# Products of 256 columns paired into products of 512 in the FFNs and the MLP of a two-block transformer on one core

## The chip, the cores and the metric

The kernel runs on one core of a Trainium2 chip. The metric is the device time of one execution in microseconds, the median of several runs. Everything is computed in one launch; all inputs and the output are float32 in HBM.

## The reference

The input is one sequence of 256 tokens of width 1024. Two blocks follow each other. The first has sliding-window, top-k and memory attention, gates, and an MLP. The second has four SwiGLU FFNs, a gated chunk mixer and a sparse attention. The change touches only the MLP and the FFNs:

```python
h = rmsnorm(x, g_mlp[l])
hid = jnp.square(jax.nn.relu(jnp.einsum("bsd,df->bsf", h, w_mlp_in[l])))      # 1024 -> 4096
x = x + jnp.einsum("bsf,fd->bsd", hid, w_mlp_out[l])                          # 4096 -> 1024

def swiglu(x, w1, w3, w2):                                                    # 1024 -> 2816 -> 1024, four times
    return (jax.nn.silu(x @ w1) * (x @ w3)) @ w2
```

## The kernel before, in words

**Two parts for each number.** Every large product runs on TensorE in fp32r, and each operand is held as a high part (the rounded value) and a low part (what the rounding lost). A product is the sum of three: high weight by high activation, high weight by low, low weight by high (`passes`). The activations of a stage lie transposed in SBUF in `hT_hi` and `hT_lo` (128 features x 8 slices x 256 tokens each); the hidden values in `hid_hi` and `hid_lo`.

**Units.** Weights come as units of 1 MB (128 x 2048 floats), in one fixed order (`plan_units`). SyncE loads a unit into one of 3 ring slots; ScalarE rounds it into the high part of one of 3 split slots (`round_unit`, L1622); VectorE subtracts to get the low part (`low_unit`, L2113), which frees the ring slot; TensorE uses it and then frees the split slot for the unit three later. The last unit of a stage goes into a place of its own, `two`.

**Chunks.** The MLP has 16 chunks of 256 hidden features, each FFN 11. Per chunk an FFN takes the units w1, w3 and w2, the MLP the units mu and md. TensorE runs one chunk ahead: w1(c+1), w3(c+1), then the down product w2(c), which accumulates into banks 4 to 7 over all chunks. The middle chunks run in hardware loops of 2 (FFN) or 3 (MLP) chunks. Chunk 0 of three FFNs (`TOK`) and chunks 0 and 1 of the MLP are computed tokens first and are turned on TensorE; that is not changed, nor is chunk 0 of FFN 2.

**An up product** (`up_T_split`) computes 128 hidden features for 256 tokens: for each of 8 slices of the contraction three matmuls of 256 columns with 128 x 128 weights, all into the same 256 columns of a PSUM bank. `two_streams` interleaves the first and the second 128 tokens. So an FFN chunk has 96 up matmuls of 256 columns and 24 down matmuls of 512, an MLP chunk 48 and 24. In an FFN the bank holds the w1 sums in its left half and the w3 sums in its right, and there are two such tiles per chunk, over banks 0 to 3; in the MLP both halves of one bank hold the two feature tiles of a chunk, over banks 0 to 2. Banks are handed out by `plan_tiles`; TensorE waits on `tile_read` of a bank before it opens it.

**The hidden values.** ScalarE applies Silu (or Relu) from the bank into `act_out` (`activate`, L1797). VectorE multiplies that with the bank (L2560 in the FFNs, L2476 in the MLP), casts to the high part (L2457) and subtracts for the low part (L2459), and then makes the low parts of the next units. TensorE waits on `hid_ready` before the down product.

**The end of a stage** (`down_last`): after the last up product TensorE does 12 matmuls of the chunk before and then needs the last hidden chunk. In VectorE's program the low part of the unit for the next stage (`following`) stands ahead of the last hidden chunk. In FFN 0, eight transposes (`turn_ws`) stand between the last up product and the 12 matmuls.

Of the kernel before, what the change touches and what calls it, by code (L numbers as in the profile page):

```python
# [130 lines left out]
def plan_tiles():  # L131
# [10 lines left out]
    def ffn(f):  # L142
        out = [("f", f, c, t) for c in range(FFN_CHUNKS) for t in range(2)]
        return out[0:2] + [("ht", f)] + out[2:] if f in TOK else out
# [18 lines left out]
    names += [("m", 0), ("hm", 0), ("m", 1), ("hm", 1), ("rel",)] + [("m", c) for c in range(2, MLP_CHUNKS)]  # L163
# [9 lines left out]
    names += [("cr", 1)] + [("ch", 1, m) for m in range(2)] + third[2:]  # L173
# [153 lines left out]
def two_blocks(nc, t, out):  # L327
    ctx = ExitStack()
    with ctx:
# [22 lines left out]
        hT_hi = sb("hT_hi", [P, KT, S], F32R)  # L352
        hT_lo = sb("hT_lo", [P, KT, S], F32R)
# [163 lines left out]
        act_ready, hid_rounded, hid_ready = sem("act_ready"), sem("hid_rounded"), sem("hid_ready")  # L517
        ws_ready, sgu_var, sgu_sd, v_ready = sem("ws_ready"), sem("sgu_var"), sem("sgu_sd"), sem("v_ready")
# [285 lines left out]
        def _(pe):  # L804
# [341 lines left out]
            def mlp(n):  # L1146
# [31 lines left out]
                def chunk(c):  # L1178
                    have(("mu", c + 1))
                    o = open_tile(("m", c + 1))  # L1180
                    for f in range(2):
                        ins = up_T_split(o[:, f * S:(f + 1) * S], parts(("mu", c + 1), KT), f * P, P)
                    owed[0] += 1
                    ins.then_inc(tile_done, 1)
                    return down(c)

                def chunk_in_turn(k, i):

                    b, held, _ = TILES[("m", MLP_BODY + k + 1)]
                    pe.wait_ge(tile_read[b], i + (held - 1))  # L1190
                    unit = split_in_turn(("mu", 1), 2 * k, i, KT)
                    for f in range(2):
                        ins = up_T_split(banks[b][:, f * S:(f + 1) * S], unit, f * P, P)
                    owed[0] += 1
                    ins.then_inc(tile_done, 1)
# [29 lines left out]
            def ffn(f, between=None):  # L1225

                def up_w1(tiles, w1):
                    for ft in range(2):
                        up_T_split(tiles[ft][:, 0:S], w1, ft * P, P)
                    owed[0] += 1  # L1230

                def up_w3(tiles, w3):
                    for ft in range(2):
                        up_T_split(tiles[ft][:, S:2 * S], w3, ft * P, P).then_inc(tile_done, 1)
                    owed[0] += 1

                def first_by_features():
# [8 lines left out]
                    up_w3(tiles, parts(("w3", f, 0), KT))  # L1246
# [30 lines left out]
                def chunk(c):  # L1277

                    have(("w1", f, c + 1))
                    tiles = [open_tile(("f", f, c + 1, ft)) for ft in range(2)]  # L1280
                    up_w1(tiles, parts(("w1", f, c + 1), KT))
# [5 lines left out]
                    up_w3(tiles, parts(("w3", f, c + 1), KT))  # L1287
# [7 lines left out]
                def chunk_in_turn(k, i):  # L1295

                    tiles = []
                    w1 = split_in_turn(("w1", f, 1), 3 * k, i, KT)
                    for ft in range(2):
                        b, held, _ = TILES[("f", f, FFN_BODY + k + 1, ft)]  # L1300
                        pe.wait_ge(tile_read[b], i + (held - 1))
                        tiles.append(banks[b])
                    up_w1(tiles, w1)
                    up_w3(tiles, split_in_turn(("w1", f, 1), 3 * k + 1, i, KT))
# [292 lines left out]
        def _(act):  # L1597
# [201 lines left out]
            def mlp():  # L1799
                first = ("mu", 1)  # L1800
                seq = TILES[("m", 2)][2] + 1 - 2
# [17 lines left out]
                relu(2)  # L1819
                round_next(first, 5)  # L1820
                round_next(first, 6)
                with act.Fori(1, turns - 1) as i:
                    for k in range(MLP_BODY):
                        activate(TILES[("m", k)][0], i * MLP_BODY + (seq + k), ACT.Relu, 2 * S)
                        round_unit(first, i, 2 * k + 1)
                        round_unit(first, i, 2 * k + 2)
                for c in range(MLP_CHUNKS - 1 - MLP_BODY, MLP_CHUNKS - 1):
                    relu(c)
# [3 lines left out]
                relu(MLP_CHUNKS - 1)  # L1832
# [1119 lines left out]
```

## Time and profile before

| what | value |
|---|---|
| median of 3 runs | 1398.87 us (1398.53 to 1399.31) |
| the profiled execution | 1398.66 us |
| its span | 1396.9 us |
| granted TensorE clock | 0.995 of full speed |
| TensorE matmul, weight load | 98 %, 91 % of the span |
| VectorE, ScalarE | 67 %, 47 % of the span |
| DMA | 268.41 MB, mean 192 GB/s |

The span is what the profile covers from the first to the last instruction; 1.8 us lie around it. An engine's share is the time in which it had an instruction running. A matmul's duration overlaps that of the next, so the rate of TensorE is read from the distance between starts, not from durations.

### The profile page before, as it was taken

The numbers are of one execution on the slowest core, as the hardware profiler recorded it, in microseconds if no ns is written. First come the engines' busy times: TensorE is split into PE (matmuls) and PEld (weight loads), VectorE is DVE, ScalarE is ACT, GpSimd is POOL, SyncE is SP. The second block draws the span as 40 slices with busy tenths as digits, with TensorE's granted clock in tenths as the row PEclk, the third lists the DMA queues.
The fourth block names the chain that finished last, engine by engine and source line by source line (L and its number), as shares of the span: only waits on it lengthen the run. The fifth ranks groups of instructions, "written<-read, shape, count | busy, mean of one in ns | idle before, by whom it ended". The sixth has DMA issues, their size and how long they took to land.

```text
span 1396.9 us, 25172 instructions
## 1 busy us (share of the span) xinstructions
PE 1364.2 (98%) x10394; PEld 1274.9 (91%) x10394; DVE 938.3 (67%) x1372; ACT 657.8 (47%) x833; POOL 76.5 (5%) x73
## 2 busy tenths in 40 slices
PE   8999989999999999999999999999999999999997
PEld 7989978999999999999889999999999887899996
DVE  6778687656675555768885556666565667765566
ACT  5666544443443444454443434444433568543432
POOL 0000150000100000000030000100000200100000
PEclk8999999999999999999999999999999999999999
DMA  8434564776658767555466656766656530566551
GB/s 284 152 122 152 196 206 154 236 237 208 214 188 249 268 206 231 181 187 176 159 217 202 203 190 217 259 216 212 210 184 207 159 135 17 182 216 205 197 195 60
DMA packets 191526, 268.41 MB, mean 192 GB/s; under 512 B 5741, under 2 KB 164753, under 8 KB 191183
## 3 DMA queue, kind: packets, MB, share of 16 engines
q1 hardware_dynamic: 186336, 250.05, 54.6%
q0 software_dynamic: 4224, 15.91, 3.3%
q10 hardware_dynamic: 878, 1.21, 0.4%
q8 instruction: 64, 1.05, 0.3%
q14 instruction: 24, 0.19, 0.0%
HBM read 261.92 MB, written 4.19 MB: 190 GB/s over the span
## 4 chain that ended last, share of the span: by engine, by line
PE 80%; DVE 12%; ACT 4%; issue 1%; DMA 1%; POOL 0%; SPq 0%; DVEq 0%; ACTq 0%
PE bank L808 79%; DVE split L2113 2%; PE bank L831 1%; DVE stats L2181 1%; DVE resid L2207 1%; DVE resid L2215 1%; ACT split L1622 1%; DMA ring<-in_w_in 1%; DVE resid L2176 1%; ACT arena L2003 1%; DVE arena L2330 0%; ACT act_out L2012 0%; DVE best L2329 0%; DVE hT_lo L2225 0%; ACT act_out L1645 0%
## 5 line engine op out<-in xcount | busy, mean ns | idle before, releaser
L2113 DVE TENSOR_TENSOR split<-ring,split 128x2048 fp32r<-128x2048 f32 x217 | 496.0, 2288 | 310.8 <-ACT split L1622 309.8
L808 PE MATMUL bank<-hT_hi,split 128*128 128x256 f32 (+1 forms) x3984 | 683.8, 276 | 1.5 <-DVE hid_lo L2491 0.7
L808 PEld LDWEIGHTS bank<-hT_hi,split 128*128 128x128 f32 (+1 forms) x3984 | 611.0, 192 | 7.9 <-issue 4.7
L1622 ACT ACTIVATE split<-ring 128x2048 fp32r<-128x2048 f32 (+1 forms) x224 | 427.1, 1908 | 297.6 <-PE bank L808 292.9
L808 PE MATMUL bank<-hT_lo,split 128*128 128x256 f32 (+1 forms) x1992 | 547.8, 275 | 0.0
L808 PEld LDWEIGHTS bank<-hT_lo,split 128*128 128x128 f32 (+1 forms) x1992 | 381.7, 192 | 1.3
L808 PE MATMUL bank<-split,hid_hi 128*128 128x512 f32 x992 | 271.2, 380 | 1.6 <-DVEq L2495 1.0
L808 PEld LDWEIGHTS bank<-split,hid_hi 128*128 128x128 f32 x992 | 183.3, 189 | 25.4 <-issue 1.9
L808 PE MATMUL bank<-split,hT_hi 128*128 128x256 f32 (+2 forms) x896 | 168.5, 290 | 2.3 <-ACT act_out L1645 0.6
L808 PE MATMUL bank<-split,hid_lo 128*128 128x512 f32 x496 | 151.4, 379 | 0.0
L808 PEld LDWEIGHTS bank<-split,hT_hi 128*128 128x128 f32 x896 | 142.2, 193 | 8.5 <-issue 4.7
L1797 ACT ACTIVATE act_out<-bank 128x256 f32<-128x256 f32 (+1 forms) x104 | 43.4, 417 | 176.9 <-PE bank L808 176.8
L808 PE MATMUL bank<-split,hT_lo 128*128 128x256 f32 (+2 forms) x448 | 126.3, 288 | 0.0
L808 PEld LDWEIGHTS bank<-split,hid_lo 128*128 128x128 f32 x496 | 93.8, 189 | 13.2
L808 PEld LDWEIGHTS bank<-split,hT_lo 128*128 128x128 f32 x448 | 86.7, 193 | 1.3
L2818 POOL TENSOR_TENSOR split<-ring,split 128x2048 fp32r<-128x2048 f32 x7 | 32.4, 4626 | 711.0 <-ACT split L1622 500.1
L2459 DVE TENSOR_TENSOR hid_lo<-hid,hid_hi 128x256 fp32r<-128x256 f32 (+1 forms) x112 | 51.4, 459 | 3.8
L808 PE MATMUL bank<-arena 64*128 64x256 f32 (+6 forms) x442 | 50.2, 321 | 1.2 <-DVE neg_max L2701 0.8
L2560 DVE SCALAR_TENSOR_TENSOR hid<-act_out,bank 128x256 f32<-128x256 f32 x82 | 37.5, 458 | 19.7 <-ACT act_out L1797 19.7
L808 PEld LDWEIGHTS bank<-arena 64*128 64x128 f32 (+3 forms) x442 | 36.6, 168 | 10.9 <-issue 3.7
L2457 DVE CAST hid_hi<-hid 128x256 fp32r<-128x256 f32 (+1 forms) x112 | 34.9, 311 | 3.9
L1677 ACT ACTIVATE hT_hi<-bank 128x512 fp32r<-128x512 f32 x28 | 16.7, 598 | 39.9 <-PE bank L831 39.9
(217 smaller groups left out, 913.8 us busy)
## 6 DMA issues: line engine op xcount, KB each, us to landing
ring<-in_ffn_w SPq DMA_DIRECT2D x132, 1024.0 KB, 5.3
ring<-in_w_in SPq DMA_DIRECT2D x19, 1024.0 KB, 5.5
ring<-in_w_mlp_in SPq DMA_DIRECT2D x16, 1024.0 KB, 5.9
ring<-in_w_mlp_out SPq DMA_DIRECT2D x16, 1024.0 KB, 5.0
ring<-in_sgu_w_in SPq DMA_DIRECT2D x16, 1024.0 KB, 5.4
ring<-in_sgu_w_out SPq DMA_DIRECT2D x8, 1024.0 KB, 4.9
ring<-in_kv_w SPq DMA_DIRECT2D x6, 1024.0 KB, 5.8
ring<-in_w_out SPq DMA_DIRECT2D x4, 1024.0 KB, 4.9
```

What stands on the lines that cost most here:

```text
L808: ins = pe.matmul(o, lhsT, rhs, start=start, stop=stop)
L831: return pe.transpose(o, a, ident[0:n, 0:n])
L1622: act.activation(halves(q if i is None else q + BODY, n)[0], ring[:, u % SLOTS, 0:n], ACT.Copy).then_inc(hi_ready, 1)
L1677: act.activation(hT_hi[:, 4 * h:4 * h + 4, b * P:(b + 1) * P], o[:, :].rearrange("p (k s) -> p k s", k=4), ACT.Copy).then_inc(hT_rounded, 1)
L1797: act.activation(act_out[:, b, 0:cols], banks[b][:, 0:cols], func).then_inc(act_ready, 1)
L2003: ins = act.activation(s, s, ACT.Exp, bias=neg_max[:, m, k:k + 1], scale=-1.0, accum_out=row_sum[:, m, k:k + 1])
L2113: dve.tensor_tensor(lo, ring[:, u % SLOTS, 0:n], hi.bitcast(F32), ALU.subtract).then_inc(split_ready, 1)
L2176: link(dve.scalar_tensor_tensor(out=r, in0=r, scalar=ALPHA if n >= 4 else 1.0, in1=from_streams(acc[2 * b + h][:, :]), op0=ALU.mult, op1=A ...
L2457: dve.tensor_copy(hi, raw).then_inc(hid_rounded, 1)
L2459: return dve.tensor_tensor(lo, raw, hi.bitcast(F32), ALU.subtract)
L2560: dve.scalar_tensor_tensor(out=in_order(raw), in0=from_streams(act_out[:, b, 0:S]), scalar=0.5, in1=from_streams(banks[b][:, S:2 * S]), op ...
L2818: pool.tensor_tensor(lo, ring[:, u % SLOTS, :], hi.bitcast(F32), ALU.subtract).then_inc(split_ready, 1)
```

## The change

In the up products of MLP chunks 2 to 15 and of FFN chunks 1 to 10, `up_T_parts` takes the place of `up_T_split`. `hT_hi` and `hT_lo` become two halves of one tensor `hT`. For each slice of the contraction there is one matmul of 512 columns, high weights by the high and the low tokens (the low ones land in the right half of the bank), and one of 256 columns, low weights by the high tokens, added to the left half. A tile so fills a whole bank with two partial sums.

VectorE adds the two halves with a `tensor_reduce` over pairs that lie 256 columns apart (`add_parts`) and writes the sum of 256 columns into `act_out`; that frees the bank. There are 28 such tiles in the MLP and 160 in the FFNs. ScalarE's Silu then works in place in `act_out`; its Relu of these chunks goes, and VectorE computes max(x, 0) times x in one instruction from SBUF. In the FFNs the adds of w1(c+1) stand in VectorE's program between the low parts of the second and the third unit of chunk c, those of w3(c) directly ahead of each half of the hidden chunk.

Cut to its core:

```diff
-    out = [("f", f, c, t) for c in range(FFN_CHUNKS) for t in range(2)]
+    first = [("f", f, 0, t) for t in range(2)]
+    rest = [(kind, f, c, t) for c in range(1, FFN_CHUNKS) for kind in ("a1", "a3") for t in range(2)]
...
-names += [("m", 0), ("hm", 0), ("m", 1), ("hm", 1), ("rel",)] + [("m", c) for c in range(2, MLP_CHUNKS)]
+names += [("m", 0), ("hm", 0), ("m", 1), ("hm", 1), ("rel",)]
+names += [("ma", c, f) for c in range(2, MLP_CHUNKS) for f in range(2)]
...
+    elif name[0] == "ma":
+        bank = (2 * name[1] + name[2]) % MLP_BODY
     elif name[0] == "hm":
-        bank = 3 - name[1]
+        bank = 0 if name[1] else 3
...
-hT_hi = sb("hT_hi", [P, KT, S], F32R)
-hT_lo = sb("hT_lo", [P, KT, S], F32R)
+hT = sb("hT", [P, 2, KT, S], F32R)
+hT_hi, hT_lo = hT[:, 0], hT[:, 1]
...
+def sums(x, ft):
+    return act_out[:, 2 * x + ft, 0:S], act_out[:, 2 * x + ft, S:2 * S]
...
+def up_T_parts(o, unit, c0):
+    for k in range(KT):
+        ins = mm(o[:, :], unit[0][:, k, c0:c0 + P],
+                 hT[:, :, k, :].rearrange("p a (t c) -> p a c t", t=2), k == 0, False)
+        if k == 0:
+            settle(ins)
+        ins = mm(o[:, 0:S], unit[1][:, k, c0:c0 + P], two_streams(hT_hi[:, k, :]), False, k == KT - 1)
+    return ins
...
-tiles = [open_tile(("f", f, c + 1, ft)) for ft in range(2)]
-up_w1(tiles, parts(("w1", f, c + 1), KT))
+up_unit("a1", c + 1, parts(("w1", f, c + 1), KT))
...
-up_w3(tiles, parts(("w3", f, c + 1), KT))
+up_unit("a3", c + 1, parts(("w3", f, c + 1), KT))
...
+def add_parts(dst, bank):
+    parts_last = bank[:, :].rearrange("p (a c t) -> p t c a", a=2, t=2)
+    return dve.tensor_reduce(in_order(dst), parts_last, AX.X, ALU.add)
...
@@ VectorE, the hidden values of an MLP chunk @@
+for f in range(2):
+    dve.wait_ge(tile_done, 2 * t0 + (seq + 1))
+    add_parts(act_out[:, x, f * S:(f + 1) * S], banks[b]).then_inc(tile_read[b], 1)
+    dve.wait_ge(tile_read[b], t2 + (held + 1))
-dve.wait_ge(act_ready, t0 + (c + 1))
-dve.tensor_tensor(halves_in_order(hid[:, x, :]), halves_from_streams(act_out[:, b, :]),
-                  halves_from_streams(banks[b][:, :]), ALU.mult).then_inc(tile_read[b], 1)
+dve.scalar_tensor_tensor(out=hid[:, x, :], in0=act_out[:, x, :], scalar=0.0, in1=act_out[:, x, :],
+                         op0=ALU.max, op1=ALU.mult).then_inc(hid_made, 1)
...
@@ VectorE, half a hidden chunk of an FFN @@
+b, read = add_tile("a3", c, ft, i)
+dve.wait_ge(tile_read[b], read)
...
+dve.scalar_tensor_tensor(out=raw, in0=s1, scalar=0.5, in1=s3, op0=ALU.mult,
+                         op1=ALU.mult).then_inc(hid_made, 1)
...
@@ VectorE, a chunk of an FFN @@
-for j in range(3 * c + 1, 3 * c + 4):
-    low_next(first, j)
+low_next(first, 3 * c + 1)
+low_next(first, 3 * c + 2)
+add_w1(c + 1)
+low_next(first, 3 * c + 3)
```

**How the rows move, first place: VectorE at the end of FFN 0** (the ends of the other FFNs read alike). Before, from the low parts of the last units (the one into `two` is w2 of the last chunk, the `split` after it belongs to the next stage) to the first row of the norm:

```order
L2113 TENSOR_TENSOR split<-ring,split 128x2048 [waits hi_ready] x2
L2113 TENSOR_TENSOR two<-ring,two 128x2048 [waits hi_ready]
L2113 TENSOR_TENSOR split<-ring,split 128x2048 [waits hi_ready]
L2560 SCALAR_TENSOR_TENSOR hid<-act_out,bank 128x256 [waits act_ready,unit_used]
L2457 CAST hid_hi<-hid 128x256 [waits tile_read2]
L2459 TENSOR_TENSOR hid_lo<-hid,hid_hi 128x256 [waits hid_rounded]
L2560 SCALAR_TENSOR_TENSOR hid<-act_out,bank 128x256 [waits act_ready]
L2457 CAST hid_hi<-hid 128x256 [waits tile_read3]
L2459 TENSOR_TENSOR hid_lo<-hid,hid_hi 128x256 [waits hid_rounded]
```

The same place in the changed kernel:

```order
L2130 TENSOR_TENSOR split<-ring,split 128x2048 [waits hi_ready] x2
L2474 TENSOR_REDUCE act_out<-bank 128x256 [waits tile_done] x2
L2130 TENSOR_TENSOR two<-ring,two 128x2048 [waits hi_ready]
L2130 TENSOR_TENSOR split<-ring,split 128x2048 [waits hi_ready]
L2474 TENSOR_REDUCE act_out<-bank 128x256 [waits tile_done]
L2613 SCALAR_TENSOR_TENSOR hid<-act_out 128x256 [waits act_ready,unit_used,tile_read2]
L2479 CAST hid_hi<-hid 128x256 [waits hid_made]
L2481 TENSOR_TENSOR hid_lo<-hid,hid_hi 128x256 [waits hid_rounded]
L2474 TENSOR_REDUCE act_out<-bank 128x256 [waits tile_done]
L2613 SCALAR_TENSOR_TENSOR hid<-act_out 128x256 [waits act_ready,tile_read3]
L2479 CAST hid_hi<-hid 128x256 [waits hid_made]
L2481 TENSOR_TENSOR hid_lo<-hid,hid_hi 128x256 [waits hid_rounded]
```

Four adds have come in: two ahead of the low part into `two`, and one ahead of each half of the last hidden chunk.

**Second place: TensorE at MLP chunk 2.** The names: `const,hid` are the transposes of hidden chunk 1, `arena` the product for the relative bias, then the first up products of chunk 2. Before:

```order
L808 MATMUL bank7<-split,hid_hi 128x512
L831 MATMUL bank2<-const,hid 128x128 [waits tile_read2,tile_read1]
L831 MATMUL bank2<-const,hid 128x128 x3
L808 MATMUL bank3<-arena 128x383 [waits tile_read3,rel_wide_ready,rel_in]
L808 MATMUL bank2<-hT_hi,split 128x256 [waits tile_read2,split_ready]
L808 MATMUL bank2<-hT_lo,split 128x256
L808 MATMUL bank2<-hT_hi,split 128x256 x2
```

In the changed kernel:

```order
L817 MATMUL bank7<-split,hid_hi 128x512
L840 MATMUL bank0<-const,hid 128x128 [waits tile_read0,tile_read1]
L840 MATMUL bank0<-const,hid 128x128 x3
L817 MATMUL bank3<-arena 128x383 [waits tile_read3,rel_wide_ready,rel_in]
L817 MATMUL bank1<-hT,split 128x512 [waits tile_read1,split_ready]
L817 MATMUL bank1<-hT,split 128x256
L817 MATMUL bank1<-hT,split 128x512
```

The transposes went from bank 2 to bank 0 and the first tile of chunk 2 from bank 2 to bank 1, so that it is no longer opened in the bank into which the transposes just wrote.

## Rows read from the trace of the kernel before

**Rows 1.** The page, parts 1 and 4: busy time, and the chain that ended last

```profile
PE 1364.2 (98%) x10394; PEld 1274.9 (91%) x10394; DVE 938.3 (67%) x1372; ACT 657.8 (47%) x833; POOL 76.5 (5%) x73
...
PE 80%; DVE 12%; ACT 4%; issue 1%; DMA 1%; POOL 0%; SPq 0%; DVEq 0%; ACTq 0%
```

**Rows 2.** Timeline of TensorE, one FFN chunk: start us, us, engine, line, op, count

```profile
479.24 0.27 PE L808 MATMUL bank<-hT_hi,split 128*128 128x256 f32 x1
...
489.96 0.60 PE L808 MATMUL bank<-split,hid_hi 128*128 128x512 f32 x2
...
495.14 0.27 PE L808 MATMUL bank<-hT_hi,split 128*128 128x256 f32 x1
```

**Rows 3.** Timeline of TensorE in the sparse attention: 16 matmuls of 32 columns

```profile
1134.67 1.97 PE L808 MATMUL bank<-arena 128*128 128x32 f32 x16
1136.48 0.36 PE L808 MATMUL bank<-hT_hi,split 128*128 128x256 f32 x1
```

**Rows 4.** Window in FFN 0: busy us (xinstructions) of PE, PEld, DVE, ACT, POOL; clock

```profile
410.00:554.00 144.00, 144.00 (x1091) 138.20 (x1090) 85.68 (x86) 59.64 (x47) 5.65 (x8) 1.00 0.72 239
```

**Rows 5.** Groups by form: busy us, mean ns of one, idle before

```profile
L2113 DVE TENSOR_TENSOR split<-ring,split 128x2048 fp32r<-128x2048 f32 x216 | 495.5, 2296 | 310.8 <-ACT split L1622 309.8 <-DVE hid_lo L2491 0.2 <-DVE hT_lo L2751 0.2
...
L2459 DVE TENSOR_TENSOR hid_lo<-hid,hid_hi 128x256 fp32r<-128x256 f32 x98 | 41.7, 426 | 3.3
...
L2457 DVE CAST hid_hi<-hid 128x256 fp32r<-128x256 f32 x98 | 28.9, 295 | 3.4
...
L2176 DVE SCALAR_TENSOR_TENSOR resid<-resid,bank 128x512 f32<-128x512 f32 x32 | 21.8, 682 | 12.6 <-PE bank L808 12.1 <-DVE stats L2181 0.3
...
L2215 DVE SCALAR_TENSOR_TENSOR resid<-resid,rstd,gain_rows 128x512 f32<-128x512 f32 x24 | 18.0, 752 | 0.8
...
L2476 DVE TENSOR_TENSOR hid<-act_out,bank 128x512 f32<-128x512 f32 x14 | 11.7, 835 | 25.9 <-ACT act_out L1797 25.9
```

**Rows 6.** Group by form: the only kind of reduction in this trace

```profile
L2717 DVE TENSOR_REDUCE cmax<-arena 128x16 f32<-128x240 f32 x2 | 0.8, 403 | 0.1
```

**Rows 7.** Timeline of VectorE at the end of FFN 1

```profile
865.75 2.29 DVE L2113 TENSOR_TENSOR split<-ring,split 128x2048 fp32r<-128x2048 f32 x1 [2.41 <-ACT split L1622]
867.96 2.28 DVE L2113 TENSOR_TENSOR two<-ring,two 128x2048 fp32r<-128x2048 f32 x1
871.21 2.29 DVE L2113 TENSOR_TENSOR split<-ring,split 128x2048 fp32r<-128x2048 f32 x1 [0.96 <-ACT split L1622]
873.41 0.44 DVE L2560 SCALAR_TENSOR_TENSOR hid<-act_out,bank 128x256 f32<-128x256 f32 x1
...
875.75 0.43 DVE L2459 TENSOR_TENSOR hid_lo<-hid,hid_hi 128x256 fp32r<-128x256 f32 x1
```

**Rows 8.** Timeline of TensorE, the same stretch

```profile
863.53 0.27 PE L808 MATMUL bank<-hT_hi,split 128*128 128x256 f32 x1
...
874.24 0.38 PE L808 MATMUL bank<-split,hid_hi 128*128 128x512 f32 x1
...
876.84 0.38 PE L808 MATMUL bank<-two,hid_hi 128*128 128x512 f32 x1
```

**Rows 9.** Timeline of TensorE at the end of FFN 0

```profile
553.56 1.04 PE L831 MATMUL bank<-const,arena 128*128 128x128 f32 x8
554.35 0.46 PE L808 MATMUL bank<-split,hid_hi 128*128 128x512 f32 x1
```

**Rows 10.** Timeline of TensorE at MLP chunk 2

```profile
231.26 0.91 PE L808 MATMUL bank<-arena 33*128 33x383 f32 x2
232.91 0.35 PE L808 MATMUL bank<-hT_hi,split 128*128 128x256 f32 x1 [0.74 <-DVE hid_lo L2491]
```

**Rows 11.** Timeline of VectorE at the start of FFN 0

```profile
406.00 0.69 DVE L2541 TENSOR_TENSOR hid_lo<-bank,hid_hi 128x512 fp32r<-128x512 f32 x1 [1.97 <-ACT hid_hi L1856]
```

**Rows 12.** Timeline of TensorE at the start of FFN 0

```profile
405.02 0.36 PE L808 MATMUL bank<-hT_hi,split 128*128 128x256 f32 x1
```

**Rows 13.** Timeline of TensorE at the end of the MLP

```profile
378.43 0.45 PE L808 MATMUL bank<-two,hid_hi 128*128 128x512 f32 x1 [0.32 <-DVE hid_lo L2459]
```

More of the change, by code:

```diff
@@ L142, in ffn @@
     def ffn(f):
-        out = [("f", f, c, t) for c in range(FFN_CHUNKS) for t in range(2)]
-        return out[0:2] + [("ht", f)] + out[2:] if f in TOK else out
+        first = [("f", f, 0, t) for t in range(2)]
+        rest = [(kind, f, c, t) for c in range(1, FFN_CHUNKS) for kind in ("a1", "a3") for t in range(2)]
+        return first + rest[0:2] + [("ht", f)] + rest[2:] if f in TOK else first + rest
     def mix(steps):
@@ L172, in plan_tiles @@
     names += [("cr", 0)] + [("ch", 0, m) for m in range(2)] + third[0:2]
-    names += [("cr", 1)] + [("ch", 1, m) for m in range(2)] + third[2:]
+    names += [("cr", 1)] + third[2:4] + [("ch", 1, m) for m in range(2)] + third[4:]
     names += half_norm(7, 0) + [("ck",), ("cv",)] + half_norm(7, 1)
@@ L1245, in first_by_features @@
                     have(("w3", f, 0))
-                    up_w3(tiles, parts(("w3", f, 0), KT))
+                    for ft in range(2):
+                        up_T_split(tiles[ft][:, S:2 * S], parts(("w3", f, 0), KT), ft * P, P).then_inc(tile_done, 1)
+                    owed[0] += 1
                     between(1)
@@ L1295, in chunk_in_turn @@
                 def chunk_in_turn(k, i):
[L1297 to L1304, printed above, removed]
+                    up_unit_in_turn("a1", k, split_in_turn(("w1", f, 1), 3 * k, i, KT), i)
+                    up_unit_in_turn("a3", k, split_in_turn(("w1", f, 1), 3 * k + 1, i, KT), i)
                     w2 = split_in_turn(("w1", f, 1), 3 * k + 2, i, 2)
@@ L2545, in low_hidden, with add_tile, add_w1, add_w1_in_turn @@
                     dve.sem_inc(hid_ready, 1)
[L2547 to L2555 removed]
+                def add_tile(kind, c, ft, i=None):
+                    b, held, seq = TILES[(kind, f, c if i is None else FFN_BODY + c, ft)]
+                    t2, t8 = (0, 0) if i is None else (i * 2, i * 4 * FFN_BODY)
+                    if i is not None:
+                        held, seq = held - 2, seq - 4 * FFN_BODY
+                    dve.wait_ge(tile_done, t8 + (seq + 1))
+                    add_parts(sums(c % FFN_BODY, ft)[kind == "a3"], banks[b]).then_inc(tile_read[b], 1)
+                    return b, t2 + (held + 1)
+                def add_w1(c):
+                    for ft in range(2):
+                        add_tile("a1", c, ft)
+                def add_w1_in_turn(k, i):
+                    for ft in range(2):
+                        add_tile("a1", k, ft, i)
+                def add_w1_of_next(i):
+                    for ft in range(2):
+                        b, _, seq = TILES[("a1", f, 2 * FFN_BODY, ft)]
+                        dve.wait_ge(tile_done, i * 4 * FFN_BODY + (seq + 1 - 4 * FFN_BODY))
+                        add_parts(sums(0, ft)[0], banks[b]).then_inc(tile_read[b], 1)
+                def rounds_of(c, ft, t4, raw):
+                    x = c % FFN_BODY
+                    ins = split_hidden(t4 + (rounded_before(f) - skipped + 2 * c + ft + 1),
+                                       (raw, hid_hi[:, x, ft], hid_lo[:, x, ft]))
+                    if ft == 1:
+                        ins.then_inc(hid_ready, 1)
+                def hidden(c, ft, i=None):
+                    t4, t6 = (0, 0) if i is None else (i * 2 * FFN_BODY, i * BODY)
+                    b, read = add_tile("a3", c, ft, i)
+                    dve.wait_ge(tile_read[b], read)
                     if ft == 0:
@@ L2580, in ffn @@
                     low_hidden()
-                    low_next(first, 3)
                 else:
                     low_unit(first)
-                    chunk(0)
+                    first_hidden(0)
+                    first_hidden(1)
+                    low_next(first, 1)
+                    low_next(first, 2)
+                add_w1(1)
+                low_next(first, 3)
                 chunk(1)
@@ L2590, in ffn @@
                         hidden(k, 1, i)
-                        for j in range(3 * k + 1, 3 * k + 4):
-                            low_unit(first, i, j)
+                        low_unit(first, i, 3 * k + 1)
+                        low_unit(first, i, 3 * k + 2)
+                        if k + 1 < FFN_BODY:
+                            add_w1_in_turn(k + 1, i)
+                        else:
+                            add_w1_of_next(i)
+                        low_unit(first, i, 3 * k + 3)
                 for c in range(FFN_CHUNKS - 1 - FFN_BODY, FFN_CHUNKS - 1):
```

81 lines of the change are left out of this document (41 added, 40 removed).

## The prediction

> **What bounds the kernel now.** I read the page first, for shares and the chain that ended last. TensorE has a matmul running for 98% of the span and 80% of the chain runs over it; VectorE stands at 67% [rows 1]. A busy share can hide slow matmuls, so next comes TensorE's timeline in one FFN chunk, for the distance between starts. The 96 up matmuls run from 479.24 to 489.96, 10.72 us, which is 111.7 ns each; the 24 down matmuls of 512 columns from 489.96 to 495.14, 5.18 us, which is 215.8 ns each [rows 2]. No idle time stands in them. The granted clock is 1.00 in this stage [rows 4], the upper level of 2.4 GHz, at which 256 columns are 106.7 ns and 512 are 213.3 ns. So TensorE is the bound, and the change pays what it takes out of TensorE's stream, as long as VectorE is in time.
>
> A matmul of 256 columns costs 5.0 ns more than its columns, one of 512 only 2.5 ns. What costs that is seen in the sparse attention: 16 matmuls of only 32 columns, with full 128 x 128 weights, take 1.81 us, 113 ns each [rows 3]. At 256 columns and below it is the load of 128 columns of weights that sets the distance, not the columns; at 512 the load fits under the stream.
>
> **What TensorE gains.** Per slice, three matmuls of 256 columns (335.0 ns) become one of 512 and one of 256 (215.8 + 111.7 = 327.5 ns): 7.5 ns less. The columns are the same, one weight load of three goes. Tiles: 14 MLP chunks x 2 and 4 FFNs x 10 chunks x 4 make 28 + 160 = 188, with 8 slices each, 1504 slices. 1504 x 7.5 ns = **11.3 us less**.
>
> [...]
>
> The matmul of 512 columns reads two pieces of SBUF that lie 2048 floats apart per partition, a pattern that no row has. Lower bound: the 215.8 ns of the down matmuls, which read one piece with the same alternation; upper bound: two matmuls of 256, 223.4 ns, and above that a loss. I take 215.8, since the jump comes once in 512 columns.
>
> **At MLP chunk 2** TensorE stands 0.74 us idle because the first tile opens the bank of the transposes of hidden chunk 1, which VectorE reads late [rows 10]. The new bank numbers take that wait away: the tile opens a bank that has been read before. The unit's low part is needed too; VectorE makes it before hidden chunk 1. **0.7 us less.**
>
> **What VectorE pays.** An add reads a whole bank (512 columns) and writes 256. The trace has no such instruction. The nearest: a reduction of 240 inputs to 16 outputs takes 403 ns [rows 6], while an elementwise instruction of 256 takes 426 ns and one of 512 that reads a bank 682 ns [rows 5]; so the time of a reduction follows its inputs, and I take 0.69 us. Bounds: 0.43 us (as if only outputs counted) and 1.38 us (half rate for pairs that lie 256 columns apart). The page "VectorE: DVE Perf Modes" of the Trainium skill, section "Rules for kernel authors", calls `tensor_reduce` the slowest VectorE operation and expects the plain rate; 0.69 us is that plain rate.
>
> In the steady state this is covered. VectorE is busy 85.68 us in 144 us [rows 4], 9.46 us per chunk of 15.90. Four adds make it 9.46 + 2.76 = 12.2 us of the new 15.66. The multiply (0.44 us) [rows 7] now reads SBUF only; I leave it the same. Latency: hidden chunk c is needed 5.18 + 2 x 5.24 = 15.7 us after w3(c) ends; two halves of add, multiply, cast, subtract take 3.9 us. Each w3 bank is opened again 10.4 us after, each w1 bank has been read before w3 of its chunk ends. ScalarE loses 14 Relus and no longer waits for w3 before Silu. The add of w1(c+1) stands ahead of the third low part, whose split slot is freed by the same end of w1(c+1) and which ScalarE has yet to round, so nothing is delayed there. In the MLP two adds replace Relu's wait and the multiply of 835 ns becomes one of about 750 (the form of L2215) [rows 5]. SyncE and the transfers: same bytes, and the ring slot of w3(c+1) frees 0.5 us later against some 5 us of slack.
>
> **At the ends of the stages** the cover is thin. At FFN 1 (T = 874.24, the end of the last up product) TensorE has 12 matmuls, 2.60 us, before it needs the last hidden chunk at 876.84 [rows 8]; VectorE finishes it at 876.18 [rows 7]. Now go through VectorE's new order. The low part of w2(9) starts 2.22 us after the last w1 product starts, so at T - 8.26 (w1 and w3 now take 10.48), and holds VectorE to T - 6.05. First add to T - 5.36. The second waits for the last w1 tile, whose last matmul starts 0.11 us before T - 5.24 and lasts 0.27 [rows 2], so that it is seen some 0.2 us after, and ends at T - 4.35. The low part into `two` runs to T - 2.2, the next stage's to T. Then twice 0.69 (add) + 0.44 + 0.30 + 0.43 with 0.03 between: the hidden chunk ends at T + 3.8, TensorE has it at T + 3.9. **A new wait of 1.3 us at FFN 1.** At FFN 0 eight transposes, 0.79 us [rows 9], stand before the same 12 matmuls: **0.5 us.** At FFN 2 the next unit has 384 columns of 2048, at FFN 3 there is none, so there VectorE is free when the last tile ends: T + 0.2 + 1.95, under 2.6, nothing. The MLP's end waits already (0.32 us) [rows 13], and Relu 0.60 + multiply 0.84 there become add 0.69 + multiply 0.75: the same.
>
> At the starts of FFN 0, 1 and 3 TensorE opens the bank of the first w1 tile again for the second w3 tile, 2.6 us after 405.02, at 407.6 [rows 12]; VectorE has hid_lo done at 406.69 [rows 11] and the add at 407.4. Held by 0.2 us, costed at nothing; each 0.1 us more per add costs up to 0.3 us in all.
>
> **Sum**, against the profiled execution of 1398.66 us (span 1396.9; 0.2 us under the median): -11.3 - 0.7 + 1.3 + 0.5 = -10.2, so **1388.5 us**.
>
> **Rivals.**
>
> Slow adds. For it: no row shows a reduction over pairs, or one from a bank; against it: the 403 ns for 240 inputs. At 1.0 us per add the waits at the ends grow from 1.8 to about 4.8 us: 1391.5. At 1.38 they are 3.8 + 3.0 + 2.1 + 1.6 at the FFNs, 0.7 at the MLP's end, 1.3 at the starts, 12.5 us: 1399.2.
>
> Slower: VectorE becomes the bound. The same price further on: four adds fill the chunk at (15.66 - 9.46) / 4 = 1.55 us each, and beyond it TensorE waits in every one of 40 FFN chunks. At 1.7 us the chunk is 16.26: 24 us there and some 15 us at ends and starts, about 1426. It loses from 1.4 us per add on. Against it: twice the rate of every row that reads a bank.
>
> A start is all that is saved. If the 112 ns of a 256-column matmul did not stay hidden in the new mix (the load for the 512-column one does not overlap as it does now), a slice would save only the 2.5 ns by which 215.8 stands above 213.3: 3.8 us, and 1398.66 - 3.8 + 1.1 = 1396.0. Against it: the 113 ns for 32 columns [rows 3]. [...]
>
> The change does not do what it says: the 512-column matmul over two pieces costs 223 ns or more. Then nothing is gained, and 1398.66 - 0.7 + 1.8 = 1399.8, no change. Against it: the matmuls now change piece at every other column already.
>
> **The numbers.** Forecast 0.78, for itself 1386.5 (no new waits) to 1390.5. Slow adds, 0.85 to 1.4 us, 0.07; a start is all 0.05; pattern costs 0.05; slower 0.05. A measurement of this kernel tells 0.2%, 2.8 us, from no change: 1395.9 to 1401.7. Faster takes the forecast and most of the slow adds, 0.84; same takes the two middle cases and the rest, 0.11; slower 0.05. The range runs from 1386.0, where every wait is covered, to 1394.5, adds of about 1.2 us.
>
> **What the new profile should show.** An FFN chunk of 15.66 us in place of 15.90, its up part 10.48 for 64 matmuls. `TENSOR_REDUCE` x188 at about 690 ns, VectorE at 75% of the span. No idle before the first matmul of MLP chunk 2. TensorE waiting on hid_lo 1.3 us at FFN 1's end, 0.5 at FFN 0's, nothing at the others. The prediction is wrong if the up part stays above 10.6 us, if adds take over 0.9 us, or if TensorE waits inside the loops.

## The result, and the profile after

| | median | runs |
|---|---|---|
| kernel before | 1399.61 us (1398.53 to 1401.48) | 17 |
| changed kernel | 1401.91 us (1400.66 to 1404.19) | 17 |
| ratio | 1.0018, 95% interval 1.0011 to 1.0026 | |

The forecast was 1388.5 us, with a range of 1386.0 to 1394.5. The changed kernel is not faster: 13.4 us above the forecast, and about 0.2% above the kernel before. The profiled execution took 1402.36 us (span 1400.6), against 1398.66 before: 3.7 us more.

The page of the changed kernel, parts 1 and 5 (part 5: busy us, mean ns of one, idle before and what ended it); [rows 1] and [rows 5] answer to it:

```profile
PE 1358.1 (97%) x8890; PEld 1228.8 (88%) x8890; DVE 1059.8 (76%) x1560; ACT 649.4 (46%) x819; POOL 78.3 (6%) x73
...
L2474 DVE TENSOR_REDUCE act_out<-bank 128x256 f32<-128x512 f32 x188 | 128.6, 686 | 20.9 <-PE bank L817 20.4
...
L2613 DVE SCALAR_TENSOR_TENSOR hid<-act_out 128x256 f32<-128x256 f32 x80 | 42.8, 535 | 9.3 <-DVE act_out L2474 5.3
```

TensorE has 1504 matmuls fewer and 6.1 us less of busy time; the 188 adds cost 686 ns each, as forecast. The odd number is the mean of the multiply, 535 ns, where its median is 426 and its maximum 4891. 80 x 0.11 us is 8.8 us too much, and all of it comes from two instructions, as will be seen.

TensorE's timeline of one FFN chunk, to hold against [rows 2]:

```profile
445.07 10.64 PE L817 MATMUL bank<-hT,split 128*128 128x512 f32 x64
455.54 0.60 PE L817 MATMUL bank<-split,hid_hi 128*128 128x512 f32 x2
...
460.73 1.47 PE L817 MATMUL bank<-hT,split 128*128 128x512 f32 x8
```

The up part is 10.47 us for 64 matmuls and the chunk 15.66, both as forecast. So the gain inside the chunks is there. It is lost at two places, the ends of FFN 0 and FFN 1 (this one execution loses 2.5 us more to a lower clock elsewhere, as the account further down shows). TensorE there, at FFN 0 and then at FFN 1 (two stretches; the second answers to [rows 8]):

```profile
552.75 0.38 PE L817 MATMUL bank<-split,hid_hi 128*128 128x512 f32 x1
557.72 0.46 PE L817 MATMUL bank<-two,hid_hi 128*128 128x512 f32 x1 [4.59 <-DVE hid_lo L2481]
...
559.61 1.06 PE L817 MATMUL bank<-two,hid_hi 128*128 128x512 f32 x2
560.46 0.64 PE L817 MATMUL bank<-two,hid_lo 128*128 128x512 f32 x1
...
876.59 0.38 PE L817 MATMUL bank<-split,hid_hi 128*128 128x512 f32 x1
882.57 0.77 PE L817 MATMUL bank<-two,hid_hi 128*128 128x512 f32 x1 [5.60 <-DVE hid_lo L2481]
```

Between the last matmul ahead of the wait and the first behind it, from start to start and less the 0.22 us of one matmul, TensorE loses 4.75 and 5.76 us, where 0.5 and 1.3 were forecast. VectorE in the same stretch of FFN 0, and the second line of FFN 1; [rows 7] answer to it:

```profile
550.19 0.42 DVE L2613 SCALAR_TENSOR_TENSOR hid<-act_out 128x256 f32<-128x256 f32 x1
550.65 0.29 DVE L2479 CAST hid_hi<-hid 128x256 fp32r<-128x256 f32 x1
550.98 0.43 DVE L2481 TENSOR_TENSOR hid_lo<-hid,hid_hi 128x256 fp32r<-128x256 f32 x1
551.32 0.68 DVE L2474 TENSOR_REDUCE act_out<-bank 128x256 f32<-128x512 f32 x1
552.04 4.75 DVE L2613 SCALAR_TENSOR_TENSOR hid<-act_out 128x256 f32<-128x256 f32 x1
...
876.75 4.89 DVE L2613 SCALAR_TENSOR_TENSOR hid<-act_out 128x256 f32<-128x256 f32 x1
```

The same instruction takes 0.42 us for the first half of the chunk and, begun 1.4 us after that one ended, 4.75 us for the second. What runs beside it is in GpSimd's timeline:

```profile
551.87 4.64 POOL L2891 TENSOR_TENSOR split<-ring,split 128x2048 fp32r<-128x2048 f32 x1 [54.42 <-ACT split L1637]
...
876.71 4.65 POOL L2891 TENSOR_TENSOR split<-ring,split 128x2048 fp32r<-128x2048 f32 x1 [154.32 <-ACT split L1637]
```

GpSimd makes the low part of the second unit of the next stage, once in each of these stages. The multiply starts 0.17 and 0.04 us behind it and ends 0.28 us after it has ended. The reduction at 551.32 reads a bank and takes its usual 0.68, but it overlaps GpSimd by only 0.13 us, which says little. In the kernel before (VectorE at the end of FFN 0, then GpSimd at both ends):

```profile
554.96 0.43 DVE L2459 TENSOR_TENSOR hid_lo<-hid,hid_hi 128x256 fp32r<-128x256 f32 x1
```

```profile
556.02 4.64 POOL L2818 TENSOR_TENSOR split<-ring,split 128x2048 fp32r<-128x2048 f32 x1 [58.86 <-ACT split L1622]
...
876.74 4.65 POOL L2818 TENSOR_TENSOR split<-ring,split 128x2048 fp32r<-128x2048 f32 x1 [156.72 <-ACT split L1622]
```

There VectorE ends its last `hid_lo` at 555.39 and 876.18 (the second in [rows 7]), about 0.6 us before GpSimd starts. The change moved VectorE's work into the time of an instruction that it had just missed.

Windows of TensorE behind the waits (us, busy us (xinstructions), granted clock, DMA share, GB/s):

```profile
556.00:558.00 2.00, 0.28 (x1) 1.00 0.18 45
558.00:560.00 2.00, 2.00 (x6) 0.53 0.93 275
560.00:562.00 2.00, 2.00 (x7) 0.62 0.61 215
562.00:564.00 2.00, 2.00 (x11) 1.00 0.00 0
```

After each long wait the granted clock falls to the lower level of 1.2 GHz, and some 8 matmuls start 427 ns apart in place of 216. From the last up product to the first product of the next stage, the two ends are 6.4 and 7.3 us longer than before, 13.8 us together; 10.5 of it are the waits, so 3.3 us are this clock.

**The first theory** from this: VectorE's multiply, which after the change reads both operands from SBUF, cannot run beside GpSimd's subtraction and waits until it has ended; then the idle TensorE pays a second time through its clock. The Trainium skill has this rule, on the page "SBUF — State Buffer", section "Who interferes with whom": a VectorE instruction with two SBUF inputs contends with a GpSimd instruction that reads SBUF, whichever comes first holds the shared ports for its whole instruction, and `tensor_reduce` never contends. By that rule the trace agrees: 4.75 us beside 4.64. A second place shows the other order: at the end of the MLP VectorE's subtraction of two SBUF operands came first (375.94 to 376.63) and took its usual 0.69 us, and GpSimd's, begun at 376.25, took 4.87 us in place of 4.64. **Rivals:** the multiply is slow by its place in `act_out`; the adds alone make VectorE late; the reductions cost something in the loops as well; the slow matmuls behind the waits come from the memories.

### The profile page after: what moved, and what is told of

Same layout as the page of the kernel before. It is cut to its first block, busy times and chain, and to the rows that moved or that the text cites. A ratio compares the mean times of both kernels' runs of the same rounds, so it can differ in the third digit from the quotient of the medians.

```text
span 1400.6 us, 22513 instructions
## 1 busy us (share of the span) xinstructions
PE 1358.1 (97%) x8890; PEld 1228.8 (88%) x8890; DVE 1059.8 (76%) x1560; ACT 649.4 (46%) x819; POOL 78.3 (6%) x73
## 4 chain that ended last, share of the span: by engine, by line
PE 79%; DVE 13%; ACT 5%; issue 1%; DMA 1%; POOL 0%; SPq 0%; DVEq 0%; ACTq 0%
PE bank L817 77%; DVE split L2130 3%; PE bank L840 1%; ACT split L1637 1%; DVE resid L2224 1%; DVE resid L2232 1%; DVE stats L2198 1%; DMA ring<-in_w_in 1%; DVE resid L2193 1%; DVE hid L2613 1%; ACT arena L2020 1%; ACT act_out L1660 1%; DVE arena L2347 0%; ACT act_out L2029 0%; DVE best L2346 0%
## 5 line engine op out<-in xcount | busy, mean ns | idle before, releaser
L817 PE MATMUL bank<-hT,split 128*128 128x512 f32 (+1 forms) x4472 | 674.1, 312 | 0.7 <-DVE split L2130 0.6
L817 PEld LDWEIGHTS bank<-hT,split 128*128 128x128 f32 x4472 | 623.9, 191 | 46.3 <-issue 3.9
L817 PE MATMUL bank<-split,hT 128*128 128x256 f32 (+2 forms) x1344 | 172.8, 288 | 3.1 <-DVE hT L2175 0.9
L817 PEld LDWEIGHTS bank<-split,hT 128*128 128x128 f32 x1344 | 163.2, 192 | 10.8 <-issue 4.5
L2474 DVE TENSOR_REDUCE act_out<-bank 128x256 f32<-128x512 f32 x188 | 128.6, 686 | 20.9 <-PE bank L817 20.4
L2613 DVE SCALAR_TENSOR_TENSOR hid<-act_out 128x256 f32<-128x256 f32 x80 | 42.8, 535 | 9.3 <-DVE act_out L2474 5.3
L817 PE MATMUL bank<-two,hid_hi 128*128 128x512 f32 x96 | 35.9, 419 | 10.5 <-DVE hid_lo L2481 10.5
L817 PEld LDWEIGHTS bank<-two,hid_hi 128*128 128x128 f32 x96 | 19.7, 205 | 14.4 <-issue 11.6
L2193 DVE SCALAR_TENSOR_TENSOR resid<-resid,bank 128x512 f32<-128x512 f32 x32 | 21.9, 683 | 13.2 <-PE bank L817 13.0
L817 PE MATMUL bank<-two,split 128*128 128x256 f32 x240 | 27.6, 276 | 0.5 <-DVEq L2457 0.5
```

Of the source, the lines that this page charges most:

```text
L817: ins = pe.matmul(o, lhsT, rhs, start=start, stop=stop)
L2193: link(dve.scalar_tensor_tensor(out=r, in0=r, scalar=ALPHA if n >= 4 else 1.0, in1=from_streams(acc[2 * b + h][:, :]), op0=ALU.mult, op1=A ...
L2474: return dve.tensor_reduce(in_order(dst), parts_last, AX.X, ALU.add)
L2613: dve.scalar_tensor_tensor(out=raw, in0=s1, scalar=0.5, in1=s3, op0=ALU.mult, op1=ALU.mult).then_inc(hid_made, 1)
```

## The experiments

Nine kernels ran. The kernel before was measured again beside them, with medians of 1400.12 us (for the first four), 1400.18 (the next four) and 1399.39 (the last), and each ratio is to that.

### GpSimd's subtraction behind the last hidden chunk

```diff
+            pool.wait_ge(hid_ready, MLP_CHUNKS + FFN_CHUNKS)
             low_unit(("sv", 1))
...
+            pool.wait_ge(hid_ready, MLP_CHUNKS + 2 * FFN_CHUNKS + 8)
             low_unit(("kv", 5))
```

> The changed kernel, with GpSimd's low part of the second unit of the next stage (at the ends of FFN 0 and FFN 1) held back until VectorE has made the last hidden chunk. Theory (VectorE's multiply L2613 has two SBUF inputs and is blocked for as long as GpSimd's subtraction of 4.65 us runs): the multiply of the last half is back at 0.43 us in place of 4.75 and 4.89 us, TensorE's idle time before the last hidden chunk falls from 4.6 and 5.6 us to about 0.5 at FFN 0 and 1.3 us at FFN 1, the half-rate matmuls after these waits go, and the time is about 1390 us. Rival (the multiply is slow by itself, or held by the weight transfers or by ScalarE's work): the 4.8 us stay, and the time stays at 1402 us.

Measured: 1389.01 us (1388.18 to 1390.42), ratio 0.9925 (0.9911 to 0.9939). At the end of FFN 1, VectorE, GpSimd and TensorE in turn:

```profile
870.31 0.42 DVE L2613 SCALAR_TENSOR_TENSOR hid<-act_out 128x256 f32<-128x256 f32 x1
```

```profile
871.60 4.65 POOL L2891 TENSOR_TENSOR split<-ring,split 128x2048 fp32r<-128x2048 f32 x1 [155.64 <-DVE hid_lo L2481]
```

```profile
870.15 0.38 PE L817 MATMUL bank<-split,hid_hi 128*128 128x512 f32 x1
871.67 0.46 PE L817 MATMUL bank<-two,hid_hi 128*128 128x512 f32 x1 [1.14 <-DVE hid_lo L2481]
```

GpSimd waits at two places, and the multiply is back at 0.42 us from the same place in `act_out`. 870.15 to 871.67 less 0.22 is a new wait of 1.3 us, the forecast's; at FFN 0 the same reading gives 0.42 (forecast 0.5). The median is 0.5 us from the forecast of the whole change, and the profiled executions compare as closely: 1388.40 against 1398.66 us is 10.3 us less, where 10.2 were forecast. So the late adds cost 1.7 us, and the overlap with GpSimd, with what followed from it, cost the rest.

### The last hidden chunk ahead of the next stage's low part

```diff
-                if following:
-                    low_unit(following)
                 hidden(FFN_CHUNKS - 1, 0)
                 hidden(FFN_CHUNKS - 1, 1)
+                if following:
+                    low_unit(following)
```

> The changed kernel, with VectorE's last hidden chunk ahead of the low part of the next stage's first unit. Theory of the port: VectorE is done with the hidden chunk 0.3 us before GpSimd can start, so TensorE does not wait at all at FFN 0 and 1, and GpSimd's subtraction (which needs the first unit's low part) starts 2.2 us later and then reaches into the norm, where it may block a VectorE instruction with two SBUF inputs (L2224) for 1 to 2 us in each of the two stages: about 1390 us. Rival (lateness alone, no port): the same order without any blocked instruction, 1388 us; and if the multiply is slow by itself, 1402 us.

Measured: 1389.78 us (1389.66 to 1390.50), ratio 0.9931 (0.9917 to 0.9945). No wait is left before the last down part. GpSimd now starts at 554.29, and what it meets is another VectorE instruction whose inputs are all in SBUF (VectorE, end of FFN 0; it takes 0.75 us otherwise):

```profile
557.99 1.49 DVE L2224 SCALAR_TENSOR_TENSOR resid<-resid,mv,gain_rows 128x512 f32<-128x512 f32 x1
```

At FFN 1 it takes 2.20 us, and TensorE stands 0.7 and 1.6 us longer before the transposes of the norm. The block moved on by one instruction; the gain is the same within the intervals.

### The last chunk of each FFN the old way

```diff
-        rest = [(kind, f, c, t) for c in range(1, FFN_CHUNKS) for kind in ("a1", "a3") for t in range(2)]
+        rest = [(kind, f, c, t) for c in range(1, FFN_CHUNKS - 1) for kind in ("a1", "a3") for t in range(2)]
+        rest += [("f", f, FFN_CHUNKS - 1, t) for t in range(2)]
...
+                    if c + 1 == FFN_CHUNKS - 1:
+                        for ft in range(2):
+                            up_T_split(tiles[ft][:, 0:S], parts(("w1", f, c + 1), KT), ft * P, P)
...
```

(with Silu and the multiply of that chunk taken from the bank, as before)

> The changed kernel, with the last chunk of every FFN made as in the kernel before (three matmuls of 256 columns, no adds, Silu and multiply from the bank). It costs TensorE 0.24 us in each of 4 chunks and takes four adds off VectorE ahead of the point where the last hidden chunk is needed. Theory (the steady state gains 0.24 us a chunk, and the loss is all at the ends of FFN 0 and 1): VectorE is in time and ahead of GpSimd, no wait over 0.1 us there, 36 FFN chunks and 14 MLP chunks keep their gain: 1399.6 - 8.6 - 1.7 - 0.7, about 1388.5 us. Rival (something else in the changed kernel costs the 12 us, spread over the stages): over 1395 us.

Measured: 1388.35 us (1387.19 to 1389.42), ratio 0.9921 (0.9908 to 0.9935). No wait at either end. VectorE in FFN 1, beside GpSimd's subtraction from 869.94 to 874.56:

```profile
871.54 0.69 DVE L2210 SCALAR_TENSOR_TENSOR resid<-resid,bank 128x512 f32<-128x512 f32 x1 [2.16 <-PE bank L818]
872.26 0.69 DVE L2215 BATCH_NORM_STATS2 stats<-resid 128x6 f32<-128x512 f32 x1
872.99 0.69 DVE L2210 SCALAR_TENSOR_TENSOR resid<-resid,bank 128x512 f32<-128x512 f32 x1
```

The same operation as the blocked multiply, but with one operand from a bank, keeps its 0.69 us beside GpSimd, twice. The norm's L2224 of the experiment above is this operation in this size with all its operands in SBUF, and it was held. So for this operation it is the second SBUF operand that matters. That the multiply itself, at its own place with an operand in the bank, would pass too was not measured.

### The kernel before, with VectorE made late

Three reductions without use stand ahead of the last hidden chunk of FFN 0 and 1 of the kernel before.

```diff
+                if f < 2:
+                    for j in range(3):
+                        dve.tensor_reduce(idle[:, 4 * f + j:4 * f + j + 1], const[:, P:K_ROW], AX.X, ALU.add)
                 hidden(FFN_CHUNKS - 1, 0)
```

> The kernel before, with three idle reductions of 545 columns on VectorE (about 2.0 us) ahead of the last hidden chunk of FFN 0 and FFN 1. Theory of the port: the multiply L2560 reads one operand from the bank and takes its 0.45 us whatever GpSimd does, but the cast or the subtraction that follows, SBUF to SBUF, meets GpSimd's subtraction and lasts over 4 us; TensorE waits some 4.5 us at FFN 0 and 5.4 at FFN 1, and the time is about 1410 us. Rival (a late VectorE costs only its lateness): waits of 0.6 and 1.3 us, about 1401.5 us.

Measured: 1412.99 us (1412.95 to 1414.15), ratio 1.0098 (1.0082 to 1.0113). VectorE at the end of FFN 0:

```profile
552.88 1.96 DVE L2600 TENSOR_REDUCE idle<-const 128x1 f32<-128x544 f32 x3
...
555.91 0.52 DVE L2561 SCALAR_TENSOR_TENSOR hid<-act_out,bank 128x256 f32<-128x256 f32 x1
556.46 4.40 DVE L2458 CAST hid_hi<-hid 128x256 fp32r<-128x256 f32 x1
```

GpSimd ran from 556.17 for 4.54 us. 2 us of delay per stage cost 13 us in all, with nothing else of the change. The multiply, with its operand in the bank, began 0.26 us before GpSimd and is not held (0.52 us for 0.43); the cast behind it is, though it has one input only, and ends 0.15 us after GpSimd. So in this stretch it would not have helped to leave one operand of the multiply in the bank. The same page and section of the Trainium skill names casts among the instructions that can take both pairs of ports; here it is 4.40 us for 0.29.

Between the two profiled executions, 14.3 us apart, the waits are 4.3 and 5.1 us, near what was expected, and the lower clock behind them costs some 5 us more: it lasted for about 12 matmuls at each end, not 8. The time is 3 us above the expected 1410.

### TensorE kept busy in the long waits

The changed kernel, with products for nobody while TensorE waits.

```diff
                 def last():
+                    if f < 2:
+                        b, held, _ = TILES[("a3", f, FFN_CHUNKS - 1, 0)]
+                        pe.wait_ge(tile_read[b], held + 1)
+                        for j in range((20, 24)[f]):
+                            mm(banks[b][:, :], hT[:, 0, j % KT, 0:P], hT[:, :, j % KT, :], True, True)
```

> The changed kernel, in which TensorE makes 20 (FFN 0) and 24 (FFN 1) products of 512 columns for nobody while it waits for the last hidden chunk, some 4.4 and 5.2 us of work in waits of 4.6 and 5.6 us. The late multiplication stays (4.75 us beside GpSimd's subtraction). Theory: the idleness itself costs a second time, because the granted clock falls after it (16 matmuls at 427 in place of 216 ns in the two stages); kept busy, TensorE keeps 2.4 GHz, no stretch below 0.9 follows, and the time is 3.4 us under the changed kernel's, 1398.5. Rival, that the slow matmuls behind the waits come from the memories or from GpSimd: they stay at 427 ns and the time is 1402 or above.

Measured: 1398.91 us (1397.25 to 1399.92), ratio 0.9990 (0.9981 to 0.9999). VectorE's multiply is late as before (4.78 and 4.91 us). TensorE at the end of FFN 0:

```profile
553.10 4.73 PE L817 MATMUL bank<-hT 128*128 128x512 f32 x20
557.88 0.45 PE L817 MATMUL bank<-two,hid_hi 128*128 128x512 f32 x1
558.17 0.38 PE L817 MATMUL bank<-two,hid_lo 128*128 128x512 f32 x1
558.39 0.59 PE L817 MATMUL bank<-two,hid_hi 128*128 128x512 f32 x2
```

And its windows there:

```profile
556.00:558.00 2.00, 1.95 (x10) 1.00 0.08 19
558.00:560.00 2.00, 2.00 (x10) 1.00 0.91 267
560.00:562.00 2.00, 2.00 (x11) 1.00 0.68 238
```

The same memory traffic (267 and 238 GB/s, against 275 and 215), the same GpSimd, the same distance across the wait (4.99 us from the last `split` matmul to the first `two`, against 4.97), but no slow matmul. The memories are out; it is the idleness. The 3.0 us between the medians (3.9 between the two ratios to the kernel before) agree with the 3.3 us read from the trace, and the slowest execution here (1399.92) is faster than the fastest of the changed kernel (1400.66).

### GpSimd's subtraction in four pieces

```diff
+                    for j in range(4):
+                        at = slice(j * n, (j + 1) * n)
+                        ins = pool.tensor_tensor(lo[:, at], ring[:, u % SLOTS, at], hi[:, at].bitcast(F32), ALU.subtract)
+                    ins.then_inc(split_ready, 1)
```

> The changed kernel with each of GpSimd's two subtractions of 2048 columns (4.65 us) written as four of 512 columns. Theory: VectorE's multiplication of two SBUF operands cannot run beside one GpSimd instruction and goes on when that instruction ends; so it lasts about 1.2 + 0.4 = 1.6 us in place of 4.75 and 4.89, the next instructions with two SBUF operands or a cast may each be held for a quarter more, and TensorE waits 2 to 4 us in place of 4.6 and 5.6: 1392 to 1399 us. If GpSimd's next quarter goes ahead of a waiting VectorE instruction, the multiplication lasts 4.7 us as before and the time is 1402. Rival, that the multiplication is slow by itself or by its place in act_out: it stays at 4.75 us.

Measured: 1398.30 us (1395.99 to 1400.77), ratio 0.9988 (0.9979 to 0.9998). VectorE at the end of FFN 0:

```profile
551.77 1.41 DVE L2613 SCALAR_TENSOR_TENSOR hid<-act_out 128x256 f32<-128x256 f32 x1
553.22 1.27 DVE L2479 CAST hid_hi<-hid 128x256 fp32r<-128x256 f32 x1
554.52 1.36 DVE L2481 TENSOR_TENSOR hid_lo<-hid,hid_hi 128x256 fp32r<-128x256 f32 x1
```

GpSimd's row is one of 5.44 us for the four:

```profile
551.60 5.44 POOL L2895 TENSOR_TENSOR split<-ring,split 128x512 fp32r<-128x512 f32 x4 [54.43 <-ACT split L1637]
```

The dose shows: with pieces a quarter as long the multiply waits about 1.0 us in place of 4.3. The two engines take turns: each of VectorE's three instructions is held once, by about 1 us, and GpSimd takes 5.44 us for what took 4.64. Cutting does not set VectorE free, it deals the wait out: TensorE still stands idle for 3.17 and 4.14 us. Its rows from the two ends (windows as above, FFN 0 and FFN 1):

```profile
556.00:558.00 2.00, 1.97 (x9) 1.00 0.00 0
...
878.00:880.00 2.00, 2.00 (x6) 0.58 0.04 8
880.00:882.00 2.00, 2.00 (x7) 0.57 0.00 0
```

After the idle 3.17 us the clock stayed, after 4.14 it fell.

### The change in the MLP alone

The kernel before, with `up_T_parts`, the new bank numbers and the adds in MLP chunks 2 to 15, the FFNs untouched.

```diff
+                        o = open_tile(("ma", c + 1, f))
+                        up_T_parts(o, parts(("mu", c + 1), KT), f * P).then_inc(tile_done, 1)
...
```

> The kernel before with the change made in the MLP's chunks 2 to 15 alone (28 tiles of 8 slices; the FFNs stay as they were). By the sum of the prediction: 224 slices x 7.5 ns = 1.7 us, and 0.7 us for the bank of chunk 2, so 2.4 us less, a ratio of 0.9983; VectorE and GpSimd share nothing there, so no multiplication of 4.8 us and no new wait. Rival, that the added reductions cost TensorE something also inside the loops: a ratio of 1.000 or above.

Measured: 1396.40 us (1395.74 to 1398.53), ratio 0.9977 (0.9968 to 0.9986); forecast 0.9983. The forecast lies inside the interval. The adds cost TensorE nothing inside the MLP's loops, and this part of the change was a gain all along; for the FFNs' loops the chunk of 15.66 us says the same. The rival falls.

### The bank of hidden chunk 1 alone

```diff
-            bank = 3 - name[1]
+            bank = 0 if name[1] else 3
```

> The kernel before with one line of the change: the hidden tile of the MLP's second chunk in bank 0 in place of 2. The idle 0.74 us ahead of the up part of chunk 2 goes, and the profile's time from chunk 2's first matmul on is 0.7 us earlier; the total is 0.7 us less, which one look cannot show, but the trace can. Rival: another wait of the same length takes its place (the unit's low part, or the bank of chunk 1), and nothing is gained.

TensorE at MLP chunk 2 of this kernel, to hold against [rows 10]:

```profile
230.90 0.91 PE L808 MATMUL bank<-arena 33*128 33x383 f32 x2
231.74 0.38 PE L808 MATMUL bank<-hT_hi,split 128*128 128x256 f32 x1
```

0.84 us in place of 1.65: 0.8 us for one number, with no other wait in its place. A single execution (1397.24 us) cannot show that in the total; the trace can.

### The old last chunk in FFN 0 and 1 alone

The kernel of the third experiment, with its condition joined by `f < 2`.

> The changed kernel with chunk 10 made the old way in FFN 0 and 1 alone; in FFN 2 and 3, where no low part of the next stage and no GpSimd work stands beside it, it keeps the products of 512 columns. Against the kernel with chunk 10 the old way in all four FFNs (1388.35) this gives back 2 x 32 slices x 7.5 ns = 0.5 us, so 1387.9, a ratio of 0.992 to the kernel before; no wait ahead of the last down part in any FFN. Rival: the paired chunk 10 costs FFN 2 or 3 an end of its own (their last hidden chunk late by the reductions), and the time is that of all four the old way or above.

Measured: 1389.29 us (1387.55 to 1390.31), ratio 0.9929 (0.9915 to 0.9942). In its trace the up part of chunk 10 is 10.48 us in FFN 2 and 3 against 10.72, so the 0.5 us are there, and no wait stands at these ends. But its profiled execution lost 1.5 us at another place, behind FFN 2 (window of this kernel first, then the same stretch of the third experiment's):

```profile
1104.00:1108.00 4.00, 4.00 (x28) 0.73 0.95 297
```

```profile
1104.00:1108.00 4.00, 4.00 (x37) 1.00 0.75 259
```

Both had idled 0.97 and 0.79 us just before, between the same instructions. The code ahead of this place differs between the two (chunk 10 of FFN 2), but that does not decide it: the changed kernel and five of its variants have the same TensorE program from FFN 2 on and the same two idle times to 0.01 us, and in their profiled executions the clock fell in three (the changed kernel, the one kept busy, this one) and stayed at 1.00 in three (the first two experiments and the four pieces). So whether the clock falls there is not decided by the code. The four repaired kernels (this one, the first three above) cannot be ranked: their intervals overlap.

## Why the prediction was wrong

**What TensorE gains: right.** The up part is 10.47 us (forecast 10.48), the chunk 15.66. The rivals "a start is all that is saved" and "the change does not do what it says" are out; the pattern over two pieces costs nothing.

**MLP chunk 2: right,** 0.8 us alone (forecast 0.7). **The adds: right,** 686 ns (forecast 0.69), VectorE at 76% (forecast 75%). **The steady state and the starts: right,** no wait in the loops; MLP alone gave 0.9977.

**"At the ends of the stages": this step failed.** Its working gave VectorE's last hidden chunk at T + 3.8 and waits of 1.3 and 0.5 us. Both are what is measured, to 0.1 us, once GpSimd is out of the way (1.30 and 0.42). What the step left out is that the second multiply, at T + 2.7, falls on GpSimd's 4.65 us, which in the kernel before began at 876.74, T + 2.5. The step looked at VectorE's and TensorE's timelines and never at GpSimd's. And the sentence "The multiply (0.44 us) [rows 7] now reads SBUF only; I leave it the same." is where the change of the operand was seen and its consequence was not: the term of 0.44 us for that multiply measured 4.75 and 4.89 us. The sum also had no term for the clock behind a wait.

The account for the profiled executions: the forecast's -10.2 us; 4.75 + 5.76 - 1.8 = 8.7 us of longer waits; 3.3 us of the lower clock behind them; and 2.5 us of lower clock at two places that the change does not touch (in its profile 0.9 us near 211 and 1.6 near 1118, absent in the profile before). Together 4.3 us more, against 3.7 measured; the other 0.6 us are small gains at four places, none above 0.3 (one of them the 0.8 us of MLP chunk 2, forecast as 0.7). The 2.5 us belong to this one execution.

**The trace of before had the sign.** VectorE, end of a stage in the kernel before, beside GpSimd's subtraction from 698.36 to 702.99:

```profile
699.56 0.69 DVE L2176 SCALAR_TENSOR_TENSOR resid<-resid,bank 128x512 f32<-128x512 f32 x1
...
701.34 2.20 DVE L2207 SCALAR_TENSOR_TENSOR resid<-resid,mv,gain_rows 128x512 f32<-128x512 f32 x1
...
1205.32 1.48 DVE L2207 SCALAR_TENSOR_TENSOR resid<-resid,mv,gain_rows 128x512 f32<-128x512 f32 x1
```

Line L2207 has a minimum of 743 ns, a median of 748 and a maximum of 2196, and the maximum ends 0.55 us after GpSimd. It reads SBUF only; its neighbour at 699.56, with a bank, is not held. The row at 1205.32 is a second case: GpSimd's subtraction there runs from 1201.61 to 1206.24, and this one ends 0.56 us after it. Even the mean showed them, 839 ns for the 24 of this line, where the same operation in the same size at L2215 has 752 [rows 5]. Had these rows been read, the price of a multiply at T + 2.7 would have been 4.9 us and not 0.44, and the forecast about 1397 us, or 1400 to 1401 with the fall of the clock, which no row of before showed after such a wait.

The rivals on the slower side asked only for slow adds. The case that came was one instruction in 80, at two places, not a rate.

## What to carry to other kernels

When a change makes an engine late or moves an operand from PSUM to SBUF, lay the timeline of every engine over the new place, GpSimd's too, and look at the maximum of a group, not only at its mean: two instructions of 4.8 us among 80 are the origin of the whole loss at the ends. Work for a later stage that GpSimd does in a quiet moment should be tied to the event that makes the moment quiet (here `hid_ready`), since it will otherwise slide onto the critical path when its neighbours move. And apply a change of a steady state to the loops, and ask separately whether the first and the last chunk can bear its latency: the best kernels here are the change with its end repaired, 1388.4 to 1389.8 us, 0.7 to 0.8% under the kernel before.

## What the runs showed of the hardware

- VectorE with two SBUF operands (multiply 4.75 and 4.89 us for 0.42, subtraction 1.36 for 0.43) or a cast (4.40 for 0.29) does not run beside a GpSimd subtraction; with an operand from a bank it does (0.69), and so do the statistics of one SBUF operand (0.69). The hold lasts to the end of the GpSimd instruction (0.15 to 0.56 us beyond it until VectorE's has ended), and between short ones the two take turns. Where VectorE came first, it took its usual 0.69 us and GpSimd 4.87 in place of 4.64.
- A wait of TensorE can cost more than its length: behind 4.59, 4.13 and 4.14 us of idleness matmuls ran at 1.2 GHz, behind 3.17 us they did not. The price was 1.6 to 1.7 us a wait in the changed kernel and 2.6 in the kernel made late; kept busy with products for nobody TensorE stayed at 2.4 GHz and the kernel was 3.0 us faster.
- The clock also fell after waits of 0.97 and 0.79 us in three executions and not in three others with the same instructions. Why is open; it is worth 1.5 to 1.6 us.
